# Gated linear attention by level pairs: only the 64 tokens that take part, in three rounds instead of four

## The reference, cut to what matters

```python
def _gla(q, k, v, gk, s0):
    ...
        b = jnp.cumsum(gc, axis=2)
        o_inter = jnp.einsum('bhcd,bhde->bhce', qc * jnp.exp(b), s)
        diff = b[:, :, :, None, :] - b[:, :, None, :, :]
        decay = jnp.exp(jnp.where(causal[:, :, None], diff, -jnp.inf))
        a = jnp.einsum('bhid,bhjd,bhijd->bhij', qc, kc, decay)
        o = o_inter + jnp.einsum('bhij,bhje->bhie', a, vc)
```

## Time and profile before

| | |
|---|---|
| median of 3 runs | 3234.21 us (3232.44 to 3240.81) |
| the profiled execution | 3232.9 us, its span 3231.2 us |
| mean granted clock of TensorE | 0.979 of full speed |
| TensorE busy in the span | 3084.7 us (95%) |
| VectorE, ScalarE, GpSimd busy | 49%, 32%, 47% |
| the stage `recurrences` | from about 431 to 890 us |

### The profile page before, as it was taken

How to read it: one execution, slowest core, us unless ns; L and a number is a source line. 1 busy time by engine, 2 the same in 40 slices (tenths; PEclk the granted TensorE clock), 3 DMA queues, 4 the chain that set the end, 5 groups by cost and what they waited for, 6 DMA issues and landing times. The chain is left out here.

```text
span 3231.2 us, 67218 instructions
## 1 busy us (share of the span) xinstructions
PE 3084.7 (95%) x28484; PEld 2894.3 (90%) x28484; DVE 1578.7 (49%) x2179; ACT 1026.8 (32%) x1834; POOL 1523.4 (47%) x1161
## 2 busy tenths in 40 slices
PE   7999977888898999999999999999999999999999
PEld 6988866777798999999999999877699999999998
DVE  5650035655666445554344433466646455543323
ACT  4222132333434332221122422256624332231212
POOL 4452143444125776764364556311126766764362
PEclk8999978999899999999999999999999999999999
DMA  6222133433661332236424343567521332238332
GB/s 208 83 79 98 49 107 103 146 101 103 205 201 53 104 108 79 91 119 247 152 85 152 93 146 124 162 219 235 161 79 58 110 97 96 77 120 303 98 137 82
DMA packets 370792, 409.45 MB, mean 127 GB/s; under 512 B 29016, under 2 KB 303537, under 8 KB 369480
## 3 DMA queue, kind: packets, MB, share of 16 engines
q1 hardware_dynamic: 363656, 380.24, 35.5%
q0 software_dynamic: 6848, 25.04, 2.5%
HBM read 272.71 MB, written 134.60 MB: 126 GB/s over the span
## 5 line engine op out<-in xcount | busy, mean ns | idle before, releaser
L864 PE MATMUL PS<-token_block,w_block 128*128 128x288 f32 x9408 | 1271.0, 297 | 13.5 <-POOL w_block L778 6.5
L864 PEld LDWEIGHTS PS<-token_block,w_block 128*128 128x128 f32 x9408 | 1262.2, 190 | 16.5 <-POOL w_block L778 6.1
L778 POOL TENSOR_TENSOR w_block<-w_pair_raw,w_block 128x512 fp32r<-128x512 f32 x224 | 302.6, 1356 | 167.0 <-ACT w_block L774 132.9
L1259 PE MATMUL PS<-act_slot,w_down_split 128*128 128x384 f32 x1872 | 328.5, 336 | 5.3 <-DMA act_slot<-act_dram 4.2
L1259 PEld LDWEIGHTS PS<-act_slot,w_down_split 128*128 128x128 f32 x1872 | 326.2, 188 | 6.9 <-DMA act_slot<-act_dram 5.2
L778 POOL TENSOR_TENSOR w_block<-w_sum,w_block 128x512 fp32r<-128x512 f32 x168 | 225.8, 1359 | 97.1 <-ACT w_block L774 97.0
L774 ACT CAST w_block<-w_pair_raw 128x512 fp32r<-128x512 f32 x224 | 137.5, 621 | 306.2 <-PE PS L864 268.5
L774 ACT CAST w_block<-w_sum 128x512 fp32r<-128x512 f32 x168 | 99.3, 620 | 366.7 <-POOL w_sum L767 235.6
L1231 PE MATMUL PS<-token_block,w_block 128*128 128x288 f32 x1344 | 180.3, 296 | 2.1 <-issue 2.1
L1231 PEld LDWEIGHTS PS<-token_block,w_block 128*128 128x128 f32 x1344 | 179.4, 189 | 2.9 <-issue 2.5
L762 POOL TENSOR_TENSOR w_sum<-w_pair_raw 128x512 f32<-128x512 f32 x56 | 88.0, 1571 | 163.6 <-DMA w_pair_raw<-in_ffn_w_gu_dram 114.8
(11 more groups left out here) (466 smaller groups left out, 5497.9 us busy)
## 6 DMA issues: line engine op xcount, KB each, us to landing
w_pair_raw<-in_ffn_w_gu_dram SPq DMA_DIRECT2D x88, 512.0 KB, 5.1
act_slot<-act_dram SPq DMA_DIRECT2D x28, 1152.0 KB, 13.3
cache_kT<-kT_dram SPq DMA_DIRECT2D x8, 2048.0 KB, 11.4
cache_v<-in_cache_c_v_dram SPq DMA_DIRECT2D x64, 256.0 KB, 4.9
act_dram<-ffn_act_high SPq DMA_DIRECT2D x28, 576.0 KB, 2.8
act_dram<-ffn_act_low SPq DMA_DIRECT2D x28, 576.0 KB, 3.9
down_source<-down_dram SPq DMA_DIRECT2D x56, 288.0 KB, 4.9
xT<-xT_dram SPq DMA_DIRECT2D x24, 576.0 KB, 12.0
```

The lines of the kernel that those rows point to most:

```text
L778: self.nc.gpsimd.tensor_tensor(self.blocks[q][:, 1], self.source(p, q), self.blocks[q][:, 0], ALU.subtract).then_inc(self.low, 1)
L864: m = nc.tensor.matmul(to[:, j], w, x[:, j * HN:(j + 1) * HN], start=(q < 3 and i == 0 and t == 0), stop=(q > 3 and i == 3 and t == 2), sk ...
L1259: m = nc.tensor.matmul(down_banks(u)[:, j], wd[u % 2][:, int(q == 2), k], x[:, int(q == 1), group(j)], start=(k == 0 and q == 0), stop=(k ...
```

## The change

Queries, products and masked copies of a level are made for the 64 tokens that take part on each side. `side(ap, j, upper)` picks the upper or the lower halves of the blocks of level j.

- Keys: for each level one GpSimd instruction of 2 x 64 elements a partition, written into the lower halves of `kl`; the upper halves stay zero, by one `memset` of 1792 elements at the start. Before: two instructions of 896 elements. The keys stay 128 columns wide, since they decide to which rows of PSUM a product goes.
- Queries: for each level one VectorE instruction of 2 x 64 elements into the now dense `ql`. Before: two of 896.
- Products: 64 columns instead of 128 for the seven levels; the diagonal keeps 128. A level takes 128 columns of a bank, so four levels fit in a round.
- Masked copies: for levels 0 to 4 two VectorE instructions of 256 elements (one for each m) instead of one of 1024.
- Rounds: prompt tiles [0, 1, 2, 3], [4, diagonal], [5, 6] instead of [0, 1], [2, 3], [4, diagonal], [5, 6]; the sample tile [0, 1], [2, 3], [diagonal] instead of [0, 1], [2], [3], [diagonal]. Its levels 4 to 6 are no longer formed. `pairs(i, 3)` and `place(i, 3)` go.

```diff
-    rounds_p, rounds_s = [[0, 1], [2, 3], [4, NL], [5, 6]], [[0, 1], [2], [3], [NL]]
+    rounds_p, rounds_s = [[0, 1, 2, 3], [4, NL], [5, 6]], [[0, 1], [2, 3], [NL]]
+    HALF = P // 2
...
-    ql = sb("gla_q_exps", [P, 2, NL, P])
+    ql = sb("gla_q_exps", [P, NL, 2, P // 2])
...
+    def side(ap, j, upper):
+        return ap.rearrange("p m (n y l) -> p m n y l", y=2, l=LEVELS[j])[:, :, :, int(upper)]
+
+    def levels(k):
+        return [j for jobs in (rounds_s if sample(k) else rounds_p) for j in jobs if j < NL]
...
-            for m in range(2):
-                x = tt_(kl[:, m], ex[:, m, 0:NL], over_heads(gkt[:, k % 2, m], NL), ALU.mult)
+            for j in levels(k):
+                x = tt_(side(kl[:, :, j], j, False), side(ex[:, :, j], j, False), side(gkt[:, k % 2], j, False), ALU.mult)
...
         spread(0)
+        nc.gpsimd.memset(kl[:], 0.0).then_inc(keys_zeroed, 1)
+        pool.wait_ge(keys_zeroed, 1)
...
-                        y = mm(PS[:, 4 + h, x * 256 + m * P:x * 256 + (m + 1) * P], w[rows], q[rows], start=True, stop=True)
+                        n = P if j == NL else HALF
+                        y = mm(PS[:, 4 + h, x * P + m * n:x * P + (m + 1) * n], w[rows], q[rows], start=True, stop=True)
...
-            if i is not None:
-                pairs(i, 3)
                 turn_w(i)
...
+                else:
+                    s = LEVELS[j]
+                    mask = side(c("up")[:, j * P:(j + 1) * P].rearrange("p (a t) -> p a t", a=1), j, True)
+                    for m in range(2):
+                        y = v.copy_predicated(side(to[:, :, m], j, True), bc(mask, (P, 4, HALF // s, s)),
+                                              src[:, :, m].rearrange("p h (n l) -> p h n l", l=s))
...
-            for m in range(2):
-                y = tt_(ql[:, m], ex[:, m, 0:NL], over_heads(gqt[:, k % 2, m], NL), ALU.mult)
+            for j in levels(k):
+                y = tt_(ql[:, j].rearrange("p m (n l) -> p m n l", l=LEVELS[j]), side(ex[:, :, j], j, True),
+                        side(gqt[:, k % 2], j, True), ALU.mult)
...
-            if i is not None:
-                place(i, 3)
-            if n is not None:
                 set_blocks(n)
```

## The result

| | before | changed |
|---|---|---|
| median | 3237.51 us (3232.44 to 3240.88, 4 runs) | 3273.97 us (3263.56 to 3278.09, 4 runs) |
| ratio, 95% interval | | 1.0114 [1.0093, 1.0135] |
| span of the profiled execution | 3231.2 us | 3261.6 us |
| mean granted clock of TensorE | 0.979 | 0.964 |

The prediction was 3230 us, 3217 to 3244. The kernel is 36.5 us slower, outside the range and on the other side.

A forecast was written before the change was run, and what follows sets the result against it. It took the pairs' products waiting for the previous round's masked copies as the longest wait, 16.5 us. Six middle turns +1.2, turn 1 -1.5, turn 0 -1.0, last turn -1.9: -3.2 together, hence 3230 us, range 3217 to 3244.

The forecast's parts named there:

- a new wait of some 0.9: Tail of a prompt turn: TensorE would wait some 0.9 us ahead of `z_half`, because `merge32` ends later.
- so the turn loses it: Front of a prompt turn: `put_level(2)` comes late, `z_blocks(2)` starts 1.7 us later, and the turn loses that.
- The tail's length: First pairs to `exponents` in a prompt turn: 15.75 us instead of 17.27, a gain of 1.5 us.
- The front: Part of a prompt turn up to the first pairs: a loss of 1.7 us through later queries and `put_level(2)`.
- The sum: All turns and the zeroing together: -3.2 us, 3232.9 to 3229.7 profiled, given as a median of 3230 us.
- Products: TensorE pairs: halving moving columns gains nothing, as spacing follows weight columns; 32 products of the first round take about 1.1 us.
- Keys: GpSimd's `level_keys`: seven instructions of 128 elements at 0.456 us each, 2.9 us in all instead of 4.12.
- The rival of cheap short instructions: GpSimd's short instructions cost only 0.30 us each, so the kernel takes 3219 us; chance 0.22.
- that of dear ones: A short GpSimd instruction costs 1.04 us, the alternation with VectorE costs more, 3249 us; chance 0.08.
- Queries: VectorE's `level_queries`: some 7.2 us from its start instead of 5.6, alternating with GpSimd's instructions.
- Copies: VectorE's masked copies: 256 elements take some 0.43 us; the first round about 3.5 us instead of 2.66.
- the dear-copies rival: Interleaved copies cost 0.64 us or more each, making the kernel slower by at least 9.7 us; chance 0.05.

The follow-up runs named there:

- experiment 1: Changed kernel with eight products of constants, adding nothing to the result, ahead of `z_half` in turns 1 to 7: 3258.92 us, ratio 1.0069.
- experiment 3: Changed kernel with `merge32` moved ahead of the first round's masked copies on VectorE: 3260.29 us, ratio 1.0086.
- experiment 7: Kernel before, with three copies of constants on VectorE between `place(i, 0)` and `merge32(i)`, making `z_half` wait: 3263.05 us, ratio 1.0077.
- experiment 8: Kernel before, with three copies of constants delaying `merge32`, and eight products of constants filling TensorE's wait ahead of `z_half`: 3258.32 us, ratio 1.0066.
- experiment 6: Changed kernel with `put_level(i, 2)` ahead of `level_queries` and eight products of constants ahead of `z_half`: 3230.82 us, ratio 0.9987.
- Experiment 4: Changed kernel with `put_level(i, 2)` moved ahead of `level_queries` on VectorE: 3246.48 us, ratio 1.0028.
- experiment 9: Changed kernel with short operands kept, the old four rounds restored, and `put_level(i, 2)` ahead of `level_queries`: 3228.49 us, ratio 0.9979.
- Experiment 2: Changed kernel with the old four rounds restored and the short keys, queries and 64 columns kept: 3252.92 us, ratio 1.0055.
- experiment 10: Kernel before, with only `put_level(i, 2)` moved ahead of `level_queries` and nothing of the change: 3232.61 us, ratio 0.9983.
- experiment 5: Changed kernel with `put_level(i, 2)` ahead of `level_queries` and `merge32` ahead of the first round's copies: 3237.27 us, ratio 1.0005.

## Why the prediction was wrong

- **The step that failed** is in the tail: "`z_half` starts at 7.2 ... so this is a new wait of some 0.9", and likewise "so the turn loses it" of `z_blocks(2)`. Both waits were foreseen, at the right places and for the right reasons. But they were booked at their own length. Nowhere did I ask what a wait does to TensorE's clock. Experiments 1, 3, 7 and 8 show it in the rows, experiment 6 against 4 in the medians. It is worth 4.9 us a turn in the profiled execution: 49.5 against the 44.6 that a turn takes when `z_half`'s wait is filled (experiment 1). Of these 29.5 us in six turns, 20.9 lie in the tails and 8.6 in the fronts, nearly all of them in i = 2 and i = 5. By the medians the filling gives back less, 15 us in experiment 1 and 13 in experiment 6, 2.5 and 2.2 for each of the six turns. Experiment 1 is still 22.7 us over the kernel before that ran beside it, and its three executions without a profile have a mean granted clock of 0.968 to 0.973, that kernel 0.974 to 0.980; in which stretches the clock fell there is not known. No rival had it.
- **The tail's length** at full clock was right: 15.75 predicted, 15.9 measured with the wait filled. It held although the first copies took longer: they began 0.3 us earlier than predicted, and VectorE's later waits took up the rest. **The front** too: 28.86 predicted (27.16 + 1.7), 28.65 measured. At full clock the six turns would be level with before, where I had +1.2 us. The sum has a slip of its own: 3229.7 and the 1.3 us to the median are 3231, not 3230.
- **Products.** 64 matmuls took 2.01 us; from start to start they were 28 ns apart, and the 32 of before 29. Halving the moving columns gave next to nothing, as the row and TensorE: Matmul & The Clock Gate in the Trainium skill, "LDWEIGHTS", both had it.
- **Keys.** 3.05 us for seven, 451 to 519 ns each, against 2.9 predicted. The rival of cheap short instructions fell, and so did that of dear ones.
- **Queries.** `level_queries` took 7.1 us, predicted 7.2. The alternation with GpSimd was read rightly. Experiment 4 adds that it is gone once GpSimd has finished.
- **Copies** were mis-sized: 3.5 us predicted for the first round, 4.25 measured, and the wait 1.72 instead of 0.9. This is a part of the dear-copies rival: on average 0.53 us each, below its threshold of 0.64. The changed kernel's copies, min/median/max ns, three of the four of the levels 0 and 1 and then three of the four of 2 and 3:

```profile
L3848 DVE COPY_PREDICATED gla_pairs<-consts_u,PS x3: 732/735/796, 685.9 to 687.3; 128x256 f32<-128x256 uint8 x3
```

```profile
L3848 DVE COPY_PREDICATED gla_pairs<-consts_u,PS x3: 425/431/440, 688.6 to 689.4; 128x256 f32<-128x256 uint8 x3
```

  The first round of two levels therefore takes 2.67 us (experiment 9), as long as the two full copies of before, 2.66. The copies save time from level 2 on.
- **The rest.** Turn i = 0 gained 0.3 (38.3 to 38.1) instead of 1.0, and i = 1 lost 1.0 (63.9 to 64.9) where I had a gain of 1.5. From the last `exponents` to `values` of the last turn it was 54.9 and is 56.0, +1.1 instead of -1.9. The mean granted clock of this stretch was 0.84 and is 0.83, so the clock hardly explains it; what does stays open. The zeroing, one instruction of 1.6 us, and what lies ahead of it moved the first `exponents` by 0.5.
- **Where the gain of a round went.** Experiment 2 answers it: with four rounds the tail takes 15.6 us, with three 15.9. The removed round had been waiting for VectorE, and VectorE has the same copies to make either way.

What stays open: the medians of experiments 7 and 8, and of 9 and 10, separate less than their profiles do. A profile is one execution, and in how many turns the clock falls may differ in the others. Which waits lower it was seen, not explained: 0.76 and 1.72 us with one group between them did, in five of six turns; 0.4 to 0.6 and 1.5 in the kernel before did, in six of six (experiment 7); 1.8 in the front did in two turns of the changed kernel, in four of experiment 2, in one of 3 and in none of 1; 1.38 ahead of the last round did in one of the six turns of the kernel before and in none of experiment 10.

One rival was not tested. In nine turns (one each of experiments 1, 2, 6 and 9, two of 4, three of 5) the clock fell at the first pairs with no wait over 0.55 us in the 7 us before, which costs some 2.5 us where nothing else is slow (experiments 1, 6 and 9). All nine are among the 48 turns with the short products; in the 24 turns with the full ones (before, experiments 7, 8 and 10), whose waits there are as short, it never did. So the short products may lower the clock by themselves. No run has them without the rest of the change.

## What to carry to other kernels

When a change gives a wait to an engine that was busy nearly throughout, price it twice: at its length, and, on TensorE, at what the following work costs at 1.2 GHz instead of 2.4; here the second was larger than every term of the sum. Judge by several executions and their mean granted clock: how often the clock falls differs from one to the next. Look for a group whose operands did not change and compare its duration: it tells the clock at once. And a chain that another engine paces does not get shorter by having one link fewer; what shortened it here was moving the instruction that others wait for ahead of the ones that nobody waits for.

## What the runs showed of the hardware that I had not expected

- TensorE went to 1.2 GHz behind waits of 0.76 and 1.72 us that stood 1.1 us of work apart, and stayed there for most of the next 14 us (granted clock 0.51), though it had no further wait in them. Products of constants in the place of the second wait kept it at 2.4 GHz there in five of six turns (experiments 1 and 6). TensorE: Matmul & The Clock Gate in the Trainium skill, "HAM oscillation — how this bites in real kernels", tells of the same effect, with waits for DMAs that are longer than these.
- A masked copy of 256 elements costs 0.73 to 0.80 us when its pattern has runs of one or two elements, and 0.42 to 0.45 with runs of four or eight. The page that the prediction cited for single words hopped over (the Vector Engine (DVE) Microarchitecture Reference of the Trainium skill, "Measured stream behaviour on trn2") has runs of two at the full rate; for these copies, with a mask of bytes and PSUM as source, runs of two were as dear as runs of one.
